# Next pair's logits moved ahead of tails and transposes, with two soft buffers and earlier gelus, in a two-block transformer kernel

## The reference

```python
# PEER, per token: 8 heads x 16 experts, one 1024-wide row u and one row v each
ue, ve = peer_u[experts], peer_v[experts]
act = gelu(einsum('td,thkd->thk', hc, ue))
y   = einsum('thk,thkd->td', g * act, ve)

# one layer of the second block (hybrid_layer), two of them
qA, kA, vA, gA, qB, kB, vB, gB, qI, kI, wI = split(x @ w_in)     # 8 + 8 heads of 64
# stick-breaking heads
z    = qA kA^T / 8
rest = where(s < t, log_sigmoid(-z), 0);  tail = reverse_cumsum(rest) - rest
oA   = where(s < t, exp(log_sigmoid(z) + tail), 0) @ vA
# sparse heads: an indexer scores the keys, the best 128 of a query stay
score = sum_h w[t,h] * relu(qI[t,h] . kI[s])
oB    = softmax(qB kB^T / 8 + rel_bias, kept keys only) @ vB
x = layer_norm(ALPHA * x + concat(oA * silu(gA), oB * silu(gB)) @ w_out)
```

## Time and profile before

| | us |
|---|---|
| three runs | 2988.78, 2983.62, 2978.09 |
| their median | 2983.62 |
| profiled execution, its own time | 2977.82 |
| its span (first to last instruction) | 2976.1 |
| stage 0, layer 0 / layer 1, from and to | 1604 to 1888 / 1888 to 2156 |
| stage 1, layer 0 / layer 1 | 2156 to 2410 / 2410 to 2660 |
| stage 2, layer 0 / layer 1 | 2660 to 2818 / 2818 to 2976 |
| PE busy over the span | 2409.9 (81%) |
| DVE busy / ACT busy | 1745.8 (59%) / 911.2 (31%) |

### The profile page before, as it was taken

The page is one execution under the profiler, slowest core; times in us unless marked ns, Lnnn a source line. Parts: engine busy times, 40 slices in busy tenths (PEclk is TensorE's granted clock), DMA queues, the critical chain, the costliest instruction groups (busy, mean ns, idle before and its releaser), DMA issues. The chain is left out here.

```text
span 2976.1 us, 30377 instructions
## 1 busy us (share of the span) xinstructions
PE 2409.9 (81%) x9779; PEld 1614.1 (54%) x9779; DVE 1745.8 (59%) x3656; ACT 911.2 (31%) x1742; POOL 982.1 (33%) x691
## 2 busy tenths in 40 slices
PE   6997999869878888898786996798557467549897
PEld 4776878758663334343333654575345345437574
DVE  3444311032136988988875678587759869865151
ACT  4444222233322222222212433143234314323232
POOL 2332555343232244344342234224323532420001
PEclk9998999989989999999898997899768778769898
DMA  4321333223139899999999899899799999965553
GB/s 158 98 67 50 96 98 102 79 83 124 52 125 343 313 407 413 415 412 397 395 414 404 325 370 356 343 365 393 303 358 373 416 406 377 386 268 196 216 190 140
DMA packets 257323, 805.56 MB, mean 271 GB/s; under 512 B 18366, under 2 KB 139862, under 8 KB 191655
## 3 DMA queue, kind: packets, MB, share of 16 engines
q0 software_dynamic: 73728, 536.90, 44.8%
q1 hardware_dynamic: 183463, 267.06, 25.6%
HBM read 795.07 MB, written 14.07 MB: 272 GB/s over the span
## 5 line engine op out<-in xcount | busy, mean ns | idle before, releaser
L1337 POOL DMA_INDIRECT gathered<-in_peer_rows,experts x436 | 530.4, 1216 | 923.5 <-DVE x_res L2630 616.3
L1695 PE MATMUL peer_banks<-gathered,peer_diags 128*128 128x512 f32 x720 | 338.3, 625 | 53.1 <-ACT peer_diags L1750 53.1
L78 PE MATMUL group_banks<-group_x_t,group_ring 128*128 128x128 f32 (+1 forms) x2016 | 342.9, 334 | 15.9 <-ACT group_x_t L2442 8.4
L78 PEld LDWEIGHTS group_banks<-group_x_t,group_ring 128*128 128x128 f32 x2016 | 310.1, 210 | 46.7 <-ACT group_x_t L2442 10.8
L2616 DVE CUSTOM_DVE_ANT_0 gathered<-gathered,late_nat 128x1024 f32<-128x1024 f32 x256 | 315.6, 1235 | 33.2 <-DMA gathered<-in_peer_rows,experts 28.1
L2630 DVE SCALAR_TENSOR_TENSOR x_res<-gathered,group_weights,x_res 128x1024 f32<-128x1024 f32 x256 | 328.3, 1283 | 2.7 <-DVE group_weights L2622 0.3
L1695 PEld LDWEIGHTS peer_banks<-gathered,peer_diags 128*128 128x128 f32 x720 | 142.5, 201 | 238.3 <-issue 238.3
L2256 PE MATMUL group_banks<-group_ring,group_x_t 128*128 128x512 f32 x512 | 235.7, 616 | 23.2 <-DMA group_ring<-in_weights 23.2
L1790 DVE CUSTOM_DVE_ANT_0 peer_product<-gathered,early_nat 128x1024 f32<-128x1024 f32 x180 | 214.7, 1223 | 37.8 <-DMA gathered<-in_peer_rows,experts 37.7
L1695 PE MATMUL peer_banks<-early_gathered,peer_diags 128*128 128x512 f32 x304 | 150.4, 647 | 53.4 <-ACT peer_diags L1750 53.4
L2256 PEld LDWEIGHTS group_banks<-group_ring,group_x_t 128*128 128x128 f32 x512 | 99.1, 198 | 146.5 <-issue 118.9
(11 more groups left out here) (376 smaller groups left out, 4211.8 us busy)
## 6 DMA issues: line engine op xcount, KB each, us to landing
group_ring<-in_weights SPq DMA_DIRECT2D x270, 512.0 KB, 6.1
mixer_wq<-in_w_in SPq DMA_DIRECT2D x24, 512.0 KB, 4.1
mixer_wk<-in_w_in SPq DMA_DIRECT2D x24, 512.0 KB, 4.1
peer_w<-in_w_pq SPq DMA_DIRECT2D x8, 1024.0 KB
gathered<-in_peer_rows,experts POOLq DMA_INDIRECT x436
diff_wv<-in_w_in SPq DMA_DIRECT2D x8, 512.0 KB, 4.1
conv_wb<-in_w_in SPq DMA_DIRECT2D x8, 512.0 KB, 4.1
merge_w<-in_w_conv_out SPq DMA_DIRECT2D x8, 512.0 KB, 3.5
```

What stands on the lines that cost most here:

```text
L78: last = nc.tensor.matmul(out, lhsT, rhs, start=n == 0, stop=n == len(pairs) - 1)
L1337: nc.gpsimd.indirect_dma_start(row_buffer(m, r), None, A["peer_rows"], bass.IndirectOffsetOnAxis(ap=at, axis=0))\
L1695: last = nc.tensor.matmul(ps[:, ACC[unit % 2] + half, :], diags[:, r % DIAGS, :], row_buffer(m, r)[:, D + half * BANK:D + (half + 1) * BAN ...
```

## The change

- **Two soft buffers.** `near_part(u)` is 0 for even and 2 for odd u: softplus writes, and soft, suffix and tails read, a buffer that alternates. `suffix` is doubled. The third part of `work` existed already.
- **PE.** The logits of pair u+1 stand directly behind its projection, ahead of `tails(u)` or `turn_weights(u)`. `stick_out` and `sparse_out` of a pair come one pair later; the gate projection of the sparse half is followed by `turn_mix(STICK)`, where `sparse_out(4)` was.
- **ACT.** `softplus(u+1)` comes ahead of `stick_weights(u)`, `copy_pair(u+1)` ahead of `sparse_weights(u)`.
- **Gelus.** `bg.lots[point]` replaces `bg.at[point]`: lots dotted by the point *in front*, though no fewer than those that DVE weighs at this point. The call stands in front of the copy, where it stood behind.

```diff
-        whole, so_far, self.at = sum(w for _, w in points), 0, {}
-        for p, w in points:
+        whole, so_far, self.at, self.lots, dotted = sum(w for _, w in points), 0, {}, {}, 0
+        for p, w in points + [("end", 0)]:
             so_far += w
             self.at[p] = self.steps * so_far // whole
-        self.at["end"] = self.steps
+            weighed = -(-max(self.at[p] - self.LAG, 0) // self.LOT)
+            self.lots[p] = max(min(dotted, self.rows) // self.LOT, min(weighed, self.rows // self.LOT))
+            dotted = self.at[p]
...
+    def near_part(u):
+        return 2 * (u % 2)
...
-        suffix = sb("suffix", [P, 2, 2 * P]) if NT == 1 else None
+        suffix = sb("suffix", [P, 2, 2, 2 * P]) if NT == 1 else None
...
                     for u in range(PAIRS):
                         pair(l, u + 1)
-                        tails(l, u)
                         if u + 1 < PAIRS:
                             stick_logits(l, u + 1)
                         else:
+                            sparse_logits(l, PAIRS)
+                        tails(l, u)
+                        if u + 1 == PAIRS:
                             natural(l, "v", SPARSE)
-                            sparse_logits(l, PAIRS)
-                        stick_out(l, u)
+                        if u:
+                            stick_out(l, u - 1)
+                    stick_out(l, PAIRS - 1)
                     for u in range(PAIRS, UNITS):
                         if u + 1 < UNITS:
                             pair(l, u + 1)
+                            sparse_logits(l, u + 1)
                         turn_weights(l, u)
-                        if u + 1 < UNITS:
-                            sparse_logits(l, u + 1)
                         if u == PAIRS:
                             natural(l, "g", SPARSE)
-                        sparse_out(l, u)
-                        if u == PAIRS:
                             turn_mix(l, STICK)
+                        else:
+                            sparse_out(l, u - 1)
+                    sparse_out(l, UNITS - 1)
...
-                    ready = min(bg.at[point], bg.rows) // bg.LOT
+                    ready = bg.lots[point]
...
                 def copy_values(l, half, done):
                     for t in tiles:
+                        done = gelus((l, f"v{half}", t), done)
                         bank = finished((l, f"v{half}", t))
                         nc.scalar.activation(values[half][:, t, :], bank, ACT.Copy).then_inc(proj_copied, 1)
-                        done = gelus((l, f"v{half}", t), done)
...
                     for u in range(PAIRS):
+                        done = gelus((l, "stick", u, 0), done)
                         copy_pair(l, u + 1)
-                        done = gelus((l, "stick", u, 0), done)
+                        if u + 1 < PAIRS:
+                            if u == 0 and searched:
+                                act.wait_ge(summed, SCORES * (l + 1))
+                            softplus(l, u + 1)
+                        done = gelus((l, "stick", u, 1), done)
                         stick_weights(l, u)
-                        done = gelus((l, "stick", u, 1), done)
-                        if u + 1 < PAIRS:
-                            softplus(l, u + 1)
-                        else:
+                        if u + 1 == PAIRS:
                             done = copy_values(l, SPARSE, done)
...
                         if p == 0:
+                            copy_pair(l, u + 1)
                             sparse_weights(l, u)
-                            copy_pair(l, u + 1)
...
```

More of the change, by code:

```diff
@@ L2307, in tails @@
                         else:
-                            later(0, suffix[:, e, 0:(last - 1) * P])
+                            later(0, suffix[:, u % 2, e, 0:(last - 1) * P])
                             made = later((last - 1) * P, soft[:, last * P:(last + 1) * P])
```

18 lines of the change are left out of this document (9 added, 9 removed).

## The result

The changed kernel takes 3004.62 us (median of 5 runs, 3000.0 to 3015.6) against 2983.62 before: a ratio of 1.0072, 95% interval 1.0051 to 1.0094. It is **slower by 21 us**, clear of the noise; the forecast was 2980.5, with a range of 2962 to 2997. The profiled execution took 3003.43 us with a span of 3001.6, 25.6 us more than the one of before.

What follows compares the result with a forecast made beforehand. The prediction took PE to bound stage 2, and DVE, with DMA engines 0.96 to 0.97 busy, stages 0 and 1. It summed -10.9 us there and +7.8 in stage 2 to -3.1: 2983.6 to 2980.5 us, range 2962 to 2997.

Steps and rivals of the forecast that it cites:

- The copies in stage 2: Stage 2, pairs 1 to 5: PE waits 0.70 us for each exposed k copy, 3.5 us a layer.
- the walk behind the gates: Stage 2, pairs 6 and 7: last DVE product comes 24.8 us behind the gate projection, where it was 23.76.
- The term of 7.8 us: Stage 2: exposed copies and a later end cost 3.9 us a layer, +7.8 us for two.
- the order in stages 0 and 1: Stages 0 and 1: the new order, with pair 5's logits moved into PE's idle time, gains; forecast at -6.7 us.
- The gelus: Stages 0 and 1: few gelus really move; net -3.0 us in layer 0 of stage 1, -0.8 at two other places.
- Rival 3: Gelus do what the change says: half of 43.2 us of DVE's waits goes, 2959 us; chance 0.05.
- The transposes of pair 4: Stage 0, layer 0: PE reaches them at 1769.2, no longer waits, starts the gate projection 0.4 us early; -2.2 us.
- Rival 2: Slower, copy exposed everywhere: stage 0 loses 2 to 3 us a layer, stage 1 gives nothing; 2996 us, chance 0.24.

Runs made afterwards that it cites:

- two_weights: Changed kernel with a second buffer for a pair's weights and transposed weights in stage 2 alone, PE's order untouched: 2985.02 us, ratio 0.9999 to before.
- two_weights_12: Changed kernel with the second weights buffer in stages 1 and 2: 2992.90 us, ratio 1.0022 to before.
- new_in_2: Kernel before with the change's gelus and soft and suffix buffers everywhere, its new PE and ACT order in stage 2 alone: 3000.08 us, ratio 1.0035.
- gelus_again: Kernel before with only the two soft buffers, doubled suffix and the change's gelus, measured a second time: 2979.50 us, ratio 0.9973.
- order_only: Changed kernel with the gelus of before, keeping the new order on PE and ACT and the two soft buffers: 3012.51 us, ratio 1.0099 to before.
- sparse_old: Changed kernel with pair 2's head product in front of the sparse values and the sparse pairs in the order of before: 2988.77 us, ratio 1.0014.
- new_in_1: Kernel before with the change's gelus and soft and suffix buffers everywhere, its new PE and ACT order in stage 1 alone: 2980.26 us, ratio 0.9983.

## Why the prediction was wrong

**The copies in stage 2: right.** "I take 0.70 us" was a little high: each wait is 0.53 or 0.54. With the buffer doubled, what remains is 2.7 and 3.5 us of idle time a layer, where the sum had 3.9.

**The step that failed** is the walk behind the gates: "brings the last DVE product 24.8 us behind the gate projection", and in it "the postponed head product of pair 6, longer by so much than the copy that it runs beside". The head product does not run beside that copy, that of pair 7. The copy writes the buffer that the product reads, and waits for it; PE then waits 1.17 us for the copy, which the walk had hidden behind the product. A pair earlier the copy of pair 6 waits in the same way for the head product of pair 5, with the exponents of pair 7 queued behind it on ACT, and PE waits 2.58 us. The walk had each engine's order and each step's inputs, but not the waits for buffers to come free. The stretch measured 27.3 to 30.0, and with the doubled buffer 23.9 and 23.7 in two_weights, a little under the 24.8 (in two_weights_12 28.0 and 23.7, the 28.0 at a granted clock of 0.86). The same omission hides the first loop: the section on stage 2 lets the head product of pair 2 stand behind 7 us of values at no charge, and puts the gate projection 2.9 us late. From the start of the values to the end of the gates the stretch was 4.5 to 6 us longer. The term of 7.8 us measured 20.6 (new_in_2 against gelus_again). These 12.8 us are about half of the miss of 24 us; the order in stages 0 and 1, forecast at -6.7 and measured at +5 to +9, is the other half, and the gelus gave back about 4.

**The clock in stage 2** was not in the sum. The new waits are short, but the clock fell where they gather. In order_only the last pairs of layer 1 (2970 to 2978) ran at 0.50 of full speed, the level of 1.2 GHz, after PE had waited 2.58 us; a wait of 1.17 followed, and the last head product took 3.67 us for 2.00 before:

```profile
2970.00:2978.00 8.00, 5.96 (x27) 5.61 (x27) 0.69 (x1) 1.02 (x1) 0.00 (x0) 0.50 0.00 0
```
```profile
2973.03 3.67 PE L78 MATMUL group_banks<-group_values,group_work 128*128 128x64 f32 x16 [1.17 <-ACT group_work L2547]
```

Of the 10.0 us that layer 1 of the changed kernel lost, 7.2 are idle time and 2.9 are busy time at the lower clock. Layer 0 lost 13.3, 6.7 idle and 6.6 busy, about 4 of these at the start of the stage. new_in_2, without that start, has 15.2 us more idle time in stage 2 than gelus_again, and 6.1 more busy time.

**The gelus: right in kind, half the size.** The order of instructions, read instead of the diff, told that most gelus do not move; that the 23.7 us turn into a wait for scores; that weights come later (13.0 to 17.6 us). Forecast were about 4 us of gain (3.0 + 0.8 in stage 1, half of 0.8 in stage 0); measured were 8.1 and 8.6, with 66.9 us of waits down to 42.9. What was missing seems to lie in stage 0. Rival 3's half of 43.2 was too much. The Trainium skill's price for a change of tables (ScalarE: Activation LUTs, "What ACT_TABLE_LOAD costs"), about 2.66 us, would bring the 3.0 of layer 0 to 5.7 by an estimate, and the sum nearer to the measured gain; but the trace of the changed kernel again starts the gelu (2198.36) 0.01 us behind the end of its load (2197.07 and 1.28), so the drain in it is not what is missing.

**The transposes of pair 4: wrong in sign.** "PE reaches the transposes at 1769.2" and starts the gate projection 0.4 us early. Less the 3.15 us by which the layer began later, it reached them at 1772.0 and started the gates 3.0 us late; in layer 1, 3.1 us late for the 2.8 early of the forecast. The lower clock was avoided as forecast (7.1 us for the first half, forecast 6.9). What the walk lacked is again the wait for the weights buffer: ACT took the exponents of pair 3 only behind the late head product, PE waited 0.96 us for them, and the head product and the projection behind took 2.19 and 8.2 us where they had taken 1.55 and 7.13. Together that is 2.7 of the 2.8 us between 1769.2 and 1772.0. Rival 2 had set the point from which it decides at 1770, and for this stage it was the right one: the order in stages 0 and 1 costs 5 to 9 us by the times, not a gain of 6.7. Its price for stage 2, the forecast's own 7.8, kept it at 2996.

**The chances.** 0.19 for slower was too little, since every case, rival 2 among them, used one number for stage 2, with bounds that came from the exposed copies alone.

## What to carry to other kernels

When a consumer is put off by one step, look up who waits for *its* end: the producer of the next step writes into the buffer that it reads, and a buffer doubled upstream moves that wait one stage on unless the ones behind are doubled as well. A walk through a new order needs three lists for each step: its engine's queue, its inputs, and the buffer it needs free. Where PE is the bound, price waits that gather higher than single ones: in new_in_2 the waits of 1.2 to 2.6 us between the short ones came with 6.1 us of slower busy time for 15.2 of idle time, while in sparse_old, whose added waits are the k copies of 0.5 us, busy time did not grow (273.2 us in stage 2, before 275.5).

## What was not expected

- PE's idle time in stage 2 repeats from run to run within a microsecond or two (18.4, 18.4 and 18.7 us in layer 0, 20.8, 20.9 and 21.3 in layer 1, in the three kernels with the same order there), while its busy time for the same 784 products ranges from 134.0 to 145.1 us with the granted clock. For the waits, two kernels are better compared by idle time than by the length of one trace; what the waits do to the clock it does not show.
- Stage 0 differs by up to 9 us between traces of the same order and gelus (542.0 us in gelus_again, 551.1 in new_in_2), stage 1 by up to 7 (492.3 in the changed kernel, 499.2 in new_in_1).
- The 162 us a layer that the prediction named for stage 2 count from rounded bounds in which a layer had 158 before. By the bounds used here it is 153 and 156, so that both layers measured near 162 is chance.
- Open: how much of the 4.6 us of stage 0 is the loop (a second buffer was not tried there), in which places the gelus gain, how much of the 19.6 us of two_weights is chance, and what brings the low clock at the start of stage 2.
